# Ordering the tokens of experts 1 to 15: a scatter to DRAM, a load back and transposes, where products with a one-hot matrix stood

## The reference, cut to what matters

```python
def _moe(h, w_router, b_router, w1, w3, w2):          # h: 256 tokens x 1024
    scores = sigmoid(h @ w_router)                      # 16 experts
    ...                                                 # best group of 4 experts, its best 2 experts
    gates = sum(one_hot(idx, 16) * wts)                 # 256 x 16, two entries per token are not zero
    out = 0
    for e in range(16):
        he = silu(h @ w1[e]) * (h @ w3[e])              # 1024 -> 512, twice
        out = out + gates[:, e:e + 1] * (he @ w2[e])    # 512 -> 1024
```

## Time and profile before

| | us |
|---|---|
| median of three runs | 1002.72 (1002.15 to 1007.28) |
| the profiled execution, its own time | 1004.23 |
| its span, first to last instruction | 1002.4 |
| PE busy in it | 942.2 (94%) |
| DVE, ACT, POOL busy | 373.4, 308.4, 31.7 |
| mean granted TensorE clock | 0.991 of full speed |
| share of PE in the chain that ended last | 84% |

### The profile page before, as it was taken

The page is one execution under the profiler, slowest core; times in us unless marked ns, Lnnn a source line. Parts: engine busy times, 40 slices in busy tenths (PEclk is TensorE's granted clock), DMA queues, the critical chain, the costliest instruction groups (busy, mean ns, idle before and its releaser), DMA issues.

```text
span 1002.4 us, 11949 instructions
## 1 busy us (share of the span) xinstructions
PE 942.2 (94%) x4380; PEld 513.4 (51%) x4381; DVE 373.4 (37%) x838; ACT 308.4 (31%) x700; POOL 31.7 (3%) x54
## 2 busy tenths in 40 slices
PE   3899989999999899997999999999989999999998
PEld 1455446546454335442355446455766456577763
DVE  1200497634271110522122321610855633236452
ACT  3211533332131121342233321311466632125420
POOL 0100200000000000000000002000000000000000
PEclk9999999999999999999999999999989999999999
DMA  9966482489696699899799999414226734423501
GB/s 349 364 212 229 50 314 99 157 297 336 215 365 229 216 334 393 297 396 396 276 398 383 398 396 295 178 48 157 85 84 239 215 93 168 161 91 101 133 19 42
DMA packets 105693, 230.75 MB, mean 230 GB/s; under 512 B 3124, under 2 KB 6504, under 8 KB 105496
## 3 DMA queue, kind: packets, MB, share of 16 engines
q1 hardware_dynamic: 100288, 217.85, 61.5%
q0 software_dynamic: 2208, 7.37, 2.6%
q10 hardware_dynamic: 3128, 4.62, 1.4%
HBM read 224.31 MB, written 5.51 MB: 229 GB/s over the span
## 4 chain that ended last, share of the span: by engine, by line
PE 84%; DVE 5%; ACT 4%; DMA 4%; issue 2%; SPq 1%; ACTq 0%; DVEq 0%
PE bank L633 24%; PE bank L900 12%; PE bank L647 9%; PE bank L913 6%; PE bank L930 4%; PE bank L599 3%; PE bank L1208 3%; DMA arena<-in_w_mod_dram 3%; PE bank L1137 3%; PE bank L1227 2%; PE bank L1218 2%; PE bank L829 1%; PE bank L925 1%; PE bank L762 1%; PE bank L983 1%
## 5 line engine op out<-in xcount | busy, mean ns | idle before, releaser
L633 PE MATMUL bank<-arena 128*128 128x512 f32 (+3 forms) x592 | 236.6, 558 | 1.9 <-DVE arena L2687 1.0
L633 PEld LDWEIGHTS bank<-arena 128*128 128x128 f32 x592 | 111.2, 190 | 117.9 <-issue 109.1
L900 PE MATMUL bank<-arena 128*64 128x512 f32 x512 | 113.0, 593 | 3.4 <-issue 3.4
L647 PE MATMUL bank<-arena 128*128 128x256 f32 (+1 forms) x384 | 99.3, 417 | 2.8 <-ACT arena L1935 1.5
L647 PEld LDWEIGHTS bank<-arena 128*128 128x128 f32 x384 | 72.1, 190 | 30.9 <-issue 21.7
L900 PEld LDWEIGHTS bank<-arena 128*64 128x64 f32 x512 | 38.8, 137 | 73.9 <-issue 73.3
L913 PE MATMUL bank<-arena,con 128*64 128x512 f32 x272 | 65.0, 621 | 4.6 <-ACT con L1838 4.0
L599 PE MATMUL bank<-arena,silu_c 128*32 128x512 f32 x384 | 48.8, 630 | 9.5 <-DMA arena<-in_w_mod_dram 6.7
L1739 ACT ACTIVATE con<-bank 128x256 f32<-128x256 f32 x17 | 6.5, 383 | 137.3 <-PE bank L900 137.3
L2358 DVE TENSOR_TENSOR con<-con,bank 128x256 f32<-128x256 f32 x17 | 7.2, 421 | 109.5 <-ACT con L1743 109.5
L913 PEld LDWEIGHTS bank<-arena,con 128*64 128x64 f32 x272 | 21.4, 143 | 37.6 <-issue 36.5
(11 more groups left out here) (409 smaller groups left out, 1209.8 us busy)
## 6 DMA issues: line engine op xcount, KB each, us to landing
arena<-in_w_gate_e_dram SPq DMA_DIRECT2D x16, 2048.0 KB, 14.0
arena<-in_w_up_e_dram SPq DMA_DIRECT2D x16, 2048.0 KB, 13.6
arena<-in_w_down_e_dram SPq DMA_DIRECT2D x16, 2048.0 KB, 12.4
arena<-in_w_mod_dram SPq DMA_DIRECT2D x12, 2048.0 KB, 12.0
arena<-in_mod_w_dram SPq DMA_DIRECT2D x12, 2048.0 KB, 8.0
arena<-in_ab_w_in_dram SPq DMA_DIRECT2D x7, 2048.0 KB, 9.6
arena<-in_gla_w_in_dram SPq DMA_DIRECT2D x6, 2048.0 KB, 11.1
arena<-in_cd_w_in_dram SPq DMA_DIRECT2D x6, 2048.0 KB, 7.9
```

Source lines behind the costliest of these rows:

```text
L633: mm = pe.matmul(ps[:, 0:n], lhs[:, k, tile * P:(tile + 1) * P], w[:, k, c0:c0 + n], start=(k == 0), stop=(k == kd_ - 1))
L647: mm = pe.matmul(ps[:, i * n:(i + 1) * n], w[:, k, c * P:(c + 1) * P], rhs[:, k, 0:n], start=(k == 0), stop=(k == KC - 1))
L900: mm = pe.matmul(up_b[64 * j:64 * j + 64, :], h[:, k, :], blocks[:, g + n:u + n + 1:u - g, :], start=(k == 0), stop=(k == KC - 1), tile_po ...
```

## The change

The one-hot products of the places 64 to 511 go, and with them the matrix's columns 64 to 511 on DVE. In their place:

- DVE turns the places into integers (`route_idx`) right behind the remaining `sel` columns and signals `slots_ready`.
- POOL scatters the token rows by these integers to a new DRAM buffer `h_rows` (512 x 1024), with four indirect DMAs (two token tiles, two choices, 512 KB each), waits until all four have landed, and loads the rows 64 to 511 back into `sorted_rows` (which lies in slot 7, over `sel`) with two DMAs of 1.5 MB and 0.25 MB. The store of `ctx_line` comes behind.
- PE turns `sorted_rows` with 32 transposes (`turn_sorted`, four per chunk, the last of each of 64 columns). This stands behind `down` of expert 0, where the gather stood ahead of `turn_ff`.
- The evictions of ACT and DVE move along: ACT's behind the two stores of expert 0, DVE's behind its product with the gate row.

```diff
@@ PE
-            def gather(other_branch=False):
-                pe.wait_ge(sel_ready, 2 * TT)
+            def turn_sorted(other_branch=False):
+                pe.wait_ge(rows_back, 16 * 2)
                 for k in range(KC):
...
-                    for t in range(TT):
-                        mm = pe.matmul(ps[:, 0:2 * T - CAP], xn2[:, t, k * P:(k + 1) * P], sel[:, t, CAP:2 * T],
-                                       start=(t == 0), stop=(t == TT - 1))
+                    for i in range(4):
+                        n = P if i < 3 else 2 * T - CAP - 3 * P
+                        mm = pe.transpose(ps[:, i * P:i * P + n], sorted_rows[0:n, i, k * P:(k + 1) * P], ident[0:n, 0:n])
                     banks.filled(name, mm)
...
                         ctx_latents(6)
-                        gather(True)
                         behind_up(e)
+                        turn_sorted(True)
@@ ACT
-                if e == 0:
-                    act.wait_ge(hg_v, 1)
-                    gather()
-                else:
+                if e:
...
                 store(y_buf[b], slot0, stored[b])
                 if e == 0:
+                    gather()
                     extras(e)
@@ DVE
-            for lo, hi in GATHERED:
-                for t in range(TT):
-                    places_in, row = iota[:, lo:hi], sel[:, t, lo:hi]
...
+            for t in range(TT):
+                row = sel[:, t, :]
...
+            dve.tensor_copy(route_idx[:, :, :], slots_ab).then_inc(slots_ready, 1)
...
                 dve.tensor_tensor(y_buf[b], dn_b[:, :], gate_rows[:, 1, 0:512], ALU.mult).then_inc(ye_ready, 1)
                 if e == 0:
+                    gather()
                     extras(e)
@@ POOL
+            pool.wait_ge(slots_ready, 1)
+            for t in range(TT):
+                for j in range(2):
+                    pool.indirect_dma_start(out=h_rows, out_offset=bass.IndirectOffsetOnAxis(ap=route_idx[:, t, j:j + 1], axis=0),
+                                            in_=xn2[:, t, :], in_offset=None).then_inc(rows_out, 16)
+            pool.wait_ge(rows_out, 16 * 4)
+            banks.wait(pool, "first5")
+            pool.dma_start(sorted_rows[:, 0:3, :], h_rows[CAP:CAP + 3 * P, :].rearrange("(t p) d -> p t d", p=P))\
+                .then_inc(rows_back, 16)
+            pool.dma_start(sorted_rows[0:2 * T - CAP - 3 * P, 3, :], h_rows[CAP + 3 * P:2 * T, :]).then_inc(rows_back, 16)
```

More of the change, by code:

```diff
@@ L264, in build @@
         hg = view(0, KC, 2 * T + CAP)
-        GATHERED = [(0, CAP), (CAP, 2 * T)]
         c_rows = mod_rows
-        sel = view(SPARE + SLOT, TT, 2 * T)
+        sel = view(SPARE + SLOT, TT, CAP)
         xn2 = view(9728, TT, D)
+        sorted_rows = view(SPARE + SLOT, 4, D)
         h2T = view(0, KC, T)
@@ L328, in slot_of @@
             return eng.value_load(flat[:, bass.ds(n, 1)], min_val=0, max_val=2 * T)
+        h_rows = nc.dram_tensor("h_rows", [2 * T, D], F32, kind="Internal").ap()
         ctx_line = nc.dram_tensor("ctx_line", [1, D], F32, kind="Internal").ap()[0]
@@ L507, in build @@
         c_ms, c_ready, c_copied = sem("c_ms"), sem("c_ready"), sem("c_copied")
+        slots_ready, rows_out, rows_back = sem("slots_ready"), sem("token_rows_out"), sem("token_rows_back")
         up_gated, x_gated, sig_step, x_sig_step = sem("up_gated"), sem("x_gated"), sem("sigmoid_step"), sem("x_sigmoid_step")
@@ L1090, in _ @@
                         ctx_latents(6)
-                        gather()
                         behind_up(e)
+                        turn_sorted()
                         extras(e)
@@ L2323, in _ @@
             link(dve.tensor_scalar(slots_ab[:, :, 0], slots_ab[:, :, 0], big, None, ALU.add))
-            for lo, hi in GATHERED:
-                for t in range(TT):
-                    places_in, row = iota[:, lo:hi], sel[:, t, lo:hi]
-                    link(dve.tensor_scalar(row, places_in, slots_ab[:, t, 0:1], None, ALU.is_equal))
-                    dve.scalar_tensor_tensor(row, places_in, slots_ab[:, t, 1:2], row, ALU.is_equal, ALU.add)\
-                       .then_inc(sel_ready, 1)
+            for t in range(TT):
+                row = sel[:, t, :]
+                link(dve.tensor_scalar(row, iota[:, 0:CAP], slots_ab[:, t, 0:1], None, ALU.is_equal))
+                dve.scalar_tensor_tensor(row, iota[:, 0:CAP], slots_ab[:, t, 1:2], row, ALU.is_equal, ALU.add)\
+                   .then_inc(sel_ready, 1)
+            dve.tensor_copy(route_idx[:, :, :], slots_ab).then_inc(slots_ready, 1)
             for t in range(EXTRA):
@@ L2334, in _ @@
                 dve.tensor_scalar(first_slot[:, :, t], slot0, float(CAP * t), 2.0 * T, ALU.add, ALU.min)
-            dve.tensor_copy(route_idx[:, :, :], slots_ab)
             for j in range(2):
```

## The result

The changed kernel takes 1012.30 us, the median of 20 runs (1007.69 to 1016.73); the kernel before takes 1005.23 beside it (20 runs, 1002.15 to 1009.27). The ratio is 1.0072, 95% interval [1.0056, 1.0087]: slower, where 999.0 and no change that can be measured were forecast, and outside the range. The profiled execution took 1011.89 us with a span of 1010.1; before these were 1004.23 and 1002.4.

What follows compares the result with a forecast made beforehand. PE, busy 94% of the span, bounds the kernel. Removing the gather's 12.27 us, less new gaps and transposes, starts expert 1's `up` 4.5 us earlier; less 0.8 for the clock, gain 3.7: 1002.72 to 999.0, range 995.8 to 1004.5.

Steps and rivals of the forecast that it cites:

- On POOL: the `ctx_line` store, needed 300 us later: On POOL behind the new waits: the store comes later, but is needed only 300 us on, so it costs nothing.
- Nothing, and at most 0.5: At the end of expert 1's `up`: `ab1_ctx` lands at 336.7, needed at 338.0; no loss, at most 0.5 us.
- Rival D: Behind expert 1's `up`: `ab1_ctx` lands 2 us late as expert 2's weights and the rows share engines; 1001.0, chance 0.07.
- signs of being wrong: Transposes wait for DMA, clock falls longer than one `down`, `pj0` waits for a landing, or `up`-to-end is not 666.9 us.
- First gap: PE ahead of expert 0's `turn_ff`: a 3.00 us wait in place of 0.78 + 1.62, then a clock fall, `down` 5.24.
- Transposes: PE behind expert 0's `down`: 32 transposes at 0.12 us each, 4.5 us in all against the gather's 12.27.
- Second gap: PE ahead of expert 1's `up`: a new 2.5 us wait for POOL's copy; a clock fall charged 0.8 at even odds.
- Rival A: The clock holds in both gaps, expert 1's `up` at 329.4: gain 6.1 us, 996.6, chance 0.24.
- The rows' way: The path through DRAM: scatter lands at 309, rows are back at 321.7 (316.9 to 330.3), hidden with 1 to 2 us spare.
- rival B: PE's first transpose waits for late rows, making the change slower: 1005.6, or 1009.4 with transposes at half clock; chance 0.14.
- Rival C: Transposes don't hold the clock, low from the first gap into expert 1's `up`: gain 1.0 us, 1001.7, chance 0.08.
- The rest of the kernel: From expert 1's `up` to the end: the distance stays 666.9 us, the shift carried through undiminished.

Runs made afterwards that it cites:

- e6: The changed kernel with the `ctx_line` store in the same place, turned on PE first to go out as 8 rows of 512 bytes: 1001.62 us, ratio 0.9980.
- e10: The changed kernel with the `ctx_line` store at its place as 128 pieces of 32 bytes, not 1024 of 4: 1003.68 us, ratio 1.0001.
- e2: The changed kernel with the `ctx_line` store moved far behind, after expert 15's stage, issued at 576.1: 1011.06 us, ratio 1.0075.
- e5: The changed kernel with the `ctx_line` store held on POOL until `ab1_ctx` has landed, issued at 339.70: 1003.28 us, ratio 0.9994.
- e4: The kernel before with only the `ctx_line` store moved later, to 310.77, and no scatter or load back: 1007.00 us, ratio 1.0026.
- e3: The kernel before with only its one-hot gather moved behind expert 0's `down`, no scatter or load back: 1012.47 us, ratio 1.0081.
- e8: e6 with both gaps covered by reordered PE and ACT work and `ab1_ctx` ahead of expert 2's `w_down`; run twice: 996.64 and 997.94 us, ratios 0.9926 and 0.9933.
- e9: e8 with a fourth tile of 128 rows in place of 64, so all transposes have one shape: 999.41 us, ratio 0.9943.
- e1: The changed kernel with the `ctx_line` store put ahead of the scatter: 1010.31 us, ratio 1.0064.
- e7: e6 with ACT keeping the second context latents behind expert 0's `ff` copy, so the sigmoid needn't wait: 1005.25 us, ratio 1.0007.

## Why the prediction was wrong, step by step

**The step that failed** is "On POOL: the `ctx_line` store, needed 300 us later". It priced a moved DMA by who needs it, and not by what it does to the transfers beside it. A row that could have made one ask was in the trace: 4 KB that took 11.7 us to land, longer than every landing of the earlier trace rows but the one of 12.5. It was a hint and no more: the stores of e6 and e10, which harm nothing, take 8.7 and 8.3. From that follows the second error, `ab1_ctx`: "Nothing, and at most 0.5". The wait for it cost 4.04, and the clock fell behind it, so that `pj0` took 9.82 in place of 7.13: 6.7 us together. e2, e5, e6 and e10 take away the store, its neighbours or its pieces, and the wait goes each time; e4 adds the store alone to the kernel before, and the wait comes. Rival D named this wait, at 2.0 us and 7 in 100, but gave expert 2's bytes as the cause and left the clock out. The remaining 1.1 to 1.4 us between 46.2 and the 38.4 and 38.1 of e2 and e6 are the first fall, which reached `turn_ff` and made `down` 6.15; e5 has the same with no store there, so it isn't the store's. Two of the prediction's own signs of being wrong came with it: `pj0` waits for a landing, and the distance from expert 1's `up` to the end is 1010.1 - 335.2 = 674.9 us, not 666.9.

The sum in the stretch, from one profile of each kernel: 5.0 for the place (e3), less 6.7 for the cheaper transposes, 6.7 for the wait and the fall behind it, 1.1 for the longer first fall; that gives the 6.1 measured. Of the 13.3 us between 999.0 and 1012.30, 2.5 are not the change's at all: the forecast started from a median of three runs, 1002.72, and twenty runs of the same kernel gave 1005.23.

**Without the store** the forecast's mechanism held and two sizes were off. e2, e6 and e10 gain 1.7 to 2.0 us in the stretch where 3.7 was forecast; the timed differences of e6 and e10, -2.0 and +0.1 with about 2 us of uncertainty either way, do not tell this gain from none.

- *First gap*, 3.00 forecast: 2.99, released by DVE. Right; and the fall behind it came, as chosen (`down` 5.01 to 6.22 us in the kernels that have the gap, against 5.24 forecast).
- *Transposes*, 4.5 forecast: 5.51. The 0.12 us came from 18 transposes of one shape; here every fourth has 64 rows, and the trace of e8 shows eight idle spells of 0.17 us, one for each. e9 takes the odd shape away and the pace is 0.12 again. ACT's late evictions, which the prediction worked out with care, did not set it: in e8 ACT evicts first, and the time is the same 5.51. The Trainium skill ("TensorEngine Tiling (Array Packing)", Key Properties) says that a change of tiling mode drains the engine; e8 and e9 fit that, with 0.17 us idle each time and (5.51 - 3.71) / 8 = 0.22 us in all, though no view here shows the drain itself.
- *Second gap*, 2.5 forecast: 2.50, released by POOL's copy. Right. But the fall of the clock behind it was charged at even odds, 0.8, and came in full in each of the eight kernels with this gap, `up` 8.78 to 10.08 against 7.05. Rival A (the clock holds) was given 0.24 on the strength of the one 2.56 us gap that it survived; at that place such a gap goes either way: behind 2.56 to 2.65 us there ten of the thirteen profiles show 7.09, and e3 and both of e8 8.51 to 8.71.
- *The rows' way*, R = 321.7 forecast: the last load was issued at 310.64 and took 10.4 us, back at 321.0. The scatter landed in 4.1 to 4.3 us, under the lower bound of 5.6 that was taken from loads. No transpose of the changed kernel waited for the rows. Right, and rival B stayed away, except in e1 (2.28 us; in e8 and e9, where PE comes to the transposes earlier, up to 0.43).
- *Rival C*: wrong. The transposes kept the upper level, 1.00 from 312 to 323 in e8's second run, and in the changed kernel the clock rose while they ran, 0.95 from 326 to 328 and 1.00 from 328 to 332, much as the 40 of before ran at 1.00. The sentence of the Trainium skill ("TensorE: Matmul & The Clock Gate", Part 4: PE-mode transpose) that the prediction weighed does not agree with these rows.
- *The rest of the kernel*: unchanged from expert 1's `turn_ff` on (652.4 us against 653.0). Counted from expert 1's `up`, as the prediction did, it grew by the wait and the slower products.

What stays open: e1's timed loss is 0.8 us more at its lower end than its stretch shows; and why the store of 1024 pieces holds back other queues' transfers, and whether by their number, their size or their addresses, no run here shows.

## What to carry to other kernels

Price a moved DMA twice: by who waits for it, and by what it does to the transfers that it now runs beside; a small one that is cut into very small pieces, here 1024 of 4 bytes, can hold others back, and the same bytes in 8 or 128 pieces did not. A gain upstream of a load that stands in a queue is worth only the load's slack: e7 and e9 saved 4.6 and 1.8 us on PE and paid more than that to `ab1_ctx`, clock included. Where a covered wait is uncovered, charge the gap and the slower product behind it, and move work into the gap, as e8 does.

## What the runs showed of the hardware

- 4 KB stored as 1024 elements of 4 bytes took 10.4 to 16.0 us to land in the kernels that have it. Where other loads ran beside it, they fell from some 400 GB/s to 86 to 174 in the change (320 to 328), to 155 and then 224 in e2 (580 to 592), to 122 to 204 in e4 (316 to 328). As 128 pieces of 32 bytes it took 8.3 us, as 8 rows of 512 bytes 8.7, with 352 to 389 GB/s beside it.
- An indirect scatter of 128 rows of 4 KB took POOL 0.95 to 1.04 us to issue, and 3.6 to 4.4 us to land where little else ran; beside the store of 1024 elements (e1) it took 9.2 to 9.8.
- A transpose of 64 rows between those of 128 came with 0.17 us idle (e8), and 32 transposes took 5.51 us with eight of them, 3.71 without (e9).
- PE's gaps of 2.28 to 4.04 us in this stretch were each followed by a stretch granted 0.50; gaps of 1.70 and less in e8 by none; the gap of 1.62 by one in the kernel before and by none in e4. Near 480 us, gaps of 2.56 to 2.65 were followed by the full clock in ten of thirteen profiles.
